# Two diffusion blocks on one core: diagonals of reciprocal sums in three attentions, and transposes of the weights in row halves in all four

## The chip, the core and the metric

The program runs on one core of one Trainium2 chip, as a single launch. The metric is the device time in microseconds of the whole program, the median over its runs. On the core, TensorE (PE) multiplies matrices and writes to PSUM, VectorE (DVE) and ScalarE (ACT) do the element-wise work, GpSimd (POOL) does a little of it, and SyncE (SP) issues most of the transfers. Each engine works through its own list of instructions in order and waits on semaphores.

## The reference, cut to what matters

Two blocks of two layers each are computed one behind the other, all in float32. Each layer holds one attention, four in all: a global one with grouped keys ("even"), one with a window and a sink ("odd"), one with low-rank keys ("mla") and a neighbourhood attention ("na"). All four have this core:

```python
def attend(q, k, v):
    s = jnp.einsum('bqhgd,bkhd->bhgqk', q, k).astype(jnp.float32)
    p = jax.nn.softmax(s, axis=-1).astype(v.dtype)
    return jnp.einsum('bhgqk,bkhd->bqhgd', p, v)
```

The odd one adds a mask and a sink column to the softmax; na adds a table of biases:

```python
    s = softmax_with_sink(jnp.concatenate([s_win, s_ctx], axis=-1))
    ...
    logits = jnp.concatenate([s_loc.reshape(B, H, GRID_W, n_loc), s_ctx], axis=-1)
    p = jax.nn.softmax(logits, axis=-1).astype(v.dtype)
```

There are 256 latent tokens and 256 context tokens. Heads have 64 channels.

## The kernel before

The feed-forward and projection stages multiply weights that stream in from HBM, each split into a high and a low part (three products, L522 to L524; in some stages two, L530 to L533). They take most of the time and aren't touched.

An attention is worked off in units. A unit (`attention_pairs`) is 128 queries of two heads: 16 units for even, odd and mla, 8 for na. Its keys are 256 or 512 (even and mla: 8 units of either), 384 (odd) or 512 (na). A unit passes through these steps, and the code of every engine loops over `it`, with different steps of different units in one iteration:

- scores, TensorE, L1519, unit `it`: two products, one for each head b, into banks 0 to 3; in even, odd and na they contract over 64 channels, head 0 in the rows 0 to 63 of the array and head 1 in rows 64 to 127; in mla over 128;
- row maximum, VectorE, L1577, unit `it` (odd and na first add mask or bias, L1571 and L1575);
- exponential, ScalarE, L1654, with the sums of the rows;
- reciprocal of the sums and scaling of the weights by it, VectorE, `scale_weights`, unit `it - 1`: L1598, then two TENSOR_SCALAR at L1602 over all keys; its last one lets TensorE go on (`probs_scaled`);
- transposes of the weights, TensorE, L1530, unit `it - 2`: one for each head and each block of 128 keys, so 4, 6 or 8, each 128x128, against an identity. Head b goes to bank 4 + b;
- copy of both banks to SBUF, ScalarE, L1640; it also gates the next unit's transposes (`turned_copied`), since the two banks aren't doubled;
- product of values and weights ("mix"), TensorE, L1548, unit `it - 3`, and the copy of its result (L1617 on VectorE, L1630 on ScalarE for odd), which the mix of a later unit waits for.

In the order of TensorE an iteration is scores of `it`, transposes of `it - 2`, mix of `it - 3`. A float32 product appears in the trace as two MATMUL instructions, each with its own weight load; a transpose is one.

Other work shares the stretches. Beside the even attention VectorE and ScalarE prepare the decays of the recurrent layer (L2677, L2683, L2529 to L2531). The odd one runs beside the last eight projection tiles (24 products of 256 columns each) with their splits (L422, L427) and rotations (L1793, L1817 to L1823), and its last part beside the first output tiles (L532, L533). Behind the attentions TensorE goes on with the recurrent layers (from L2335 and L3384 on) or the output projection.

The shapes on the array matter below: the trace writes 64*128 for a product that contracts over 64 rows and has 128 output rows, 128*64 for the mixes, 128*128 for the rest. L2414, in the recurrent layer, already transposes in row halves, and L3384 has float32 products of 64 rows with 128 columns of weights and 128 moving columns.

## Time and profile before

| | us |
|---|---|
| Median of 3 runs | 2491.78 (2486.28 to 2492.4) |
| The profiled execution, its own time | 2487.92 |
| Its span | 2486.1 |
| TensorE busy in the span | 2385.2 (96%) |
| VectorE busy | 1712.9 (69%) |
| ScalarE busy | 1062.8 (43%) |
| Even attention, first scores to the next layer's first product | 50.8 |
| Odd attention with the projection tiles beside it | 78.4 |
| MLA attention | 53.3 |
| Neighbourhood attention | 35.2 |

A busy TensorE isn't one at its peak: products are pipelined and their ends are modelled. Where it is busy all the time, the distance between the starts of two groups says what a group costs. The chain that ended last lies on TensorE for 83% of the span and on VectorE for 8%.

### The profile page before, as it was taken

To read this page: it belongs to the slowest core of one execution; us is meant where nothing else is said; L and a number is where in the kernel's file an instruction comes from. 1 tells how busy PE (TensorE), PEld (TensorE's weight loads), DVE (VectorE), ACT (ScalarE), POOL (GpSimd) and SP (SyncE) were. 2 spreads that over 40 slices of the span, in tenths; PEclk is the share of its full clock that TensorE was granted. 3 is DMA by queue.
4 is the path that set the end of the run, shared out by engine and by line. 5 is a ranking of instruction groups with operands and counts; after the bars stand their busy time and mean duration, and the time that the engine had idled before them with its cause. 6 is when DMAs were issued, how large, how long until landed. Compare 5 with 4: busy or idle time off the path is not lost.

```text
span 2486.1 us, 45211 instructions
## 1 busy us (share of the span) xinstructions
PE 2385.2 (96%) x17410; PEld 1922.4 (77%) x17410; DVE 1712.9 (69%) x2826; ACT 1062.8 (43%) x1748; POOL 380.5 (15%) x350
## 2 busy tenths in 40 slices
PE   6999999998888999999999999989999999999998
PEld 4888888866776878888788888767888885678877
DVE  3877787666565787778887763687777324776666
ACT  4232224356444622322523222475556334656354
POOL 2000001022444200000100001101002711211052
PEclk9999999999999999999999999999999999999999
DMA  7655663210000365566465553315564222113311
GB/s 294 225 194 191 194 201 125 93 39 3 4 4 19 104 215 194 192 194 203 144 216 193 191 176 99 109 38 161 186 184 138 90 97 91 31 52 128 117 45 52
DMA packets 89012, 324.76 MB, mean 131 GB/s; under 512 B 9888, under 2 KB 11040, under 8 KB 88096
## 3 DMA queue, kind: packets, MB, share of 16 engines
q1 hardware_dynamic: 86768, 310.15, 38.3%
q0 software_dynamic: 2096, 12.55, 1.5%
q8 instruction: 103, 1.69, 0.3%
q14 instruction: 45, 0.37, 0.0%
HBM read 321.49 MB, written 1.18 MB: 130 GB/s over the span
## 4 chain that ended last, share of the span: by engine, by line
PE 83%; DVE 8%; issue 3%; ACT 3%; DMA 1%; DVEq 1%; POOLq 0%; POOL 0%; ACTq 0%; SPq 0%
PE bank L522 20%; PE bank L523 20%; PE bank L524 20%; PE bank L532 5%; PE bank L533 3%; PE bank L1519 1%; DVE row_statistics L1577 1%; PE bank L1548 1%; PE bank L1530 1%; DMA projections<-stream_k 1%; DVE weights_hi_lo L427 1%; DVE work L1602 1%; PE bank L2414 1%; PE bank L1969 1%; PE bank L531 1%
## 5 line engine op out<-in xcount | busy, mean ns | idle before, releaser
L422 ACT ACTIVATE weights_hi_lo<-weight_ring 128x1024 fp32r<-128x1024 f32 (+1 forms) x338 | 352.2, 1042 | 992.0 <-PE bank L524 933.9
L522 PE MATMUL bank<-input_hi,weights_hi_lo 128*128 128x512 f32 (+1 forms) x1688 | 643.2, 381 | 12.3 <-DVE input_lo L866 4.5
L427 DVE TENSOR_TENSOR weights_hi_lo<-weight_ring,weights_hi_lo 128x1024 fp32r<-128x1024 f32 (+1 forms) x333 | 403.4, 1211 | 351.4 <-ACT weights_hi_lo L422 349.8
L523 PE MATMUL bank<-input_lo,weights_hi_lo 128*128 128x512 f32 (+1 forms) x1688 | 639.8, 379 | 0.0
L524 PE MATMUL bank<-input_hi,weights_hi_lo 128*128 128x512 f32 (+1 forms) x1688 | 639.5, 379 | 0.0
L522 PEld LDWEIGHTS bank<-input_hi,weights_hi_lo 128*128 128x128 f32 x1688 | 318.8, 189 | 79.0 <-issue 16.0
L524 PEld LDWEIGHTS bank<-input_hi,weights_hi_lo 128*128 128x128 f32 x1688 | 318.8, 189 | 59.6
L523 PEld LDWEIGHTS bank<-input_lo,weights_hi_lo 128*128 128x128 f32 x1688 | 318.8, 189 | 59.3 <-issue 0.7
L806 POOL TENSOR_TENSOR work<-work 128x512 f32<-128x512 f32 (+1 forms) x48 | 68.4, 1426 | 1225.2 <-ACT work L691 1224.3
L598 DVE CUSTOM_DVE_ANT_0 work<-weight_ring,extra_tiles 128x1024 f32<-128x1024 f32 x176 | 224.5, 1275 | 35.8 <-issue 13.2
L522 PE MATMUL bank<-hidden_hi_lo,weights_hi_lo 128*128 128x512 f32 x632 | 246.8, 390 | 0.0
L524 PE MATMUL bank<-hidden_hi_lo,weights_hi_lo 128*128 128x512 f32 x632 | 245.9, 389 | 0.0
L523 PE MATMUL bank<-hidden_hi_lo,weights_hi_lo 128*128 128x512 f32 x632 | 245.9, 389 | 0.0
L599 DVE CUSTOM_DVE_ANT_0 weight_ring<-weight_ring,extra_tiles 128x1024 f32<-128x1024 f32 x176 | 214.8, 1220 | 0.0
L522 PEld LDWEIGHTS bank<-hidden_hi_lo,weights_hi_lo 128*128 128x128 f32 x632 | 118.7, 188 | 25.1 <-ACT work L2780 0.2
L523 PEld LDWEIGHTS bank<-hidden_hi_lo,weights_hi_lo 128*128 128x128 f32 x632 | 118.7, 188 | 25.0 <-issue 0.5
L524 PEld LDWEIGHTS bank<-hidden_hi_lo,weights_hi_lo 128*128 128x128 f32 x632 | 118.6, 188 | 24.7
L1577 DVE TENSOR_REDUCE row_statistics<-bank 128x2 f32<-128x1024 f32 (+2 forms) x56 | 55.7, 994 | 26.2 <-PE bank L1519 24.1
L1397 DVE TENSOR_TENSOR work<-work,bank 128x512 f32<-128x512 f32 x66 | 45.4, 688 | 37.0 <-PE bank L524 32.9
L427 DVE TENSOR_TENSOR hidden_hi_lo<-weight_ring,hidden_hi_lo 128x1024 fp32r<-128x1024 f32 (+1 forms) x45 | 53.9, 1197 | 15.2 <-ACT hidden_hi_lo L422 14.9
L717 DVE SCALAR_TENSOR_TENSOR input_lo<-residual_stream,modulation,input_hi 128x256 fp32r<-128x256 f32 x96 | 58.4, 649 | 7.4 <-ACT input_hi L706 3.8
L691 ACT ACTIVATE work<-residual_stream 128x512 f32<-128x512 f32 (+1 forms) x72 | 40.9, 577 | 51.5 <-DVE residual_stream L1120 22.8
(598 smaller groups left out, 3725.2 us busy)
## 6 DMA issues: line engine op xcount, KB each, us to landing
weight_ring<-stream_k SPq DMA_DIRECT2D x481, 512.0 KB, 3.4
weight_ring<-stream_f SPq DMA_DIRECT2D x64, 448.0 KB, 3.4
weight_ring<-stream_f SPq DMA_DIRECT2D x32, 512.0 KB, 3.7
projections<-stream_k SPq DMA_DIRECT2D x14, 512.0 KB, 6.5
extra_tiles<-condrows POOLq DMA_DIRECT2D x3, 1024.0 KB, 8.2
constants<-consts POOLq DMA_DIRECT2D x1, 2112.5 KB, 8.3
residual_stream<-xin SPq DMA_DIRECT2D x1, 2048.0 KB, 10.4
work<-nabias POOLq DMA_DIRECT2D x1, 2048.0 KB, 9.3
```

The costliest lines, as they stand in the source:

```text
L422: act.activation(split_place(place)[:, 0, 0:words], w[:, 0:words], ACT.Copy).then_inc(hi_ready, 1)
L427: eng.tensor_tensor(split_place(place)[:, 1, 0:words], ring[:, n % RING, 0:words], split_place(place)[:, 0, 0:words].bitcast(F32), ALU.sub ...
L522: pe.matmul(out, weights[:, 0, w], x_hi, start=first, stop=False)
L523: pe.matmul(out, weights[:, 0, w], x_lo, start=False, stop=False)
L524: return pe.matmul(out, weights[:, 1, w], x_hi, start=False, stop=last)
L532: pe.matmul(bank[:, :], weights[:, 0, w], x_lo_hi, start=first, stop=False)
L533: return pe.matmul(bank[:, TC:T], weights[:, 1, w], x_lo_hi[:, TC:T], start=False, stop=False)
L598: dve.tensor_tensor_reduce(PRODUCTS, w, COND[:, 0, :], 1.0, 0.0, ALU.mult, ALU.add, MOD_SUMS[:, j, 0:1])
L599: dve.tensor_tensor_reduce(w, w, COND[:, 1, :], 1.0, 0.0, ALU.mult, ALU.add, MOD_SUMS[:, j, 1:2]) .then_inc(mod_read, 1)
L717: ins = dve.scalar_tensor_tensor(out=H_LO[:, kt, p:q], in0=X[:, kt, p:q], scalar=MODS[:, scale + kt, s:s + 1], in1=H_HI[:, kt, p:q].bitcas ...
L806: pool.tensor_tensor(total, total, squares_of(place, kt)[:, a:b], ALU.add)
L1577: ins = dve.tensor_reduce(st[:, 0, :], sc[:, :, 0:nk], AX.X, ALU.max, negate=True)
```

## The change

In even, odd and na the weights are no longer scaled. VectorE builds, in place of L1602, two small matrices of 128x64: each row p of matrix b holds the reciprocal of the sum of query p and head b in column p mod 64 and zeros elsewhere (the product of the two triangular masks `iu` and `il` is a stacked 64x64 identity). TensorE then multiplies the unscaled weights by it, so that turning and scaling are one product. The product contracts over queries in two halves of 64 rows: half 0 in the array's upper rows, into bank 4, half 1 in its lower rows, into bank 5, 64 moving columns each. For mla the scaling stays, and the transposes are cut into the same halves against a 64x64 part of the identity. The copy of L1640 puts the halves together again as it writes; the mix reads the same columns from a flat tile.

Per unit with n blocks (n = 4, 6 or 8 for 256, 384 or 512 keys), TensorE had n transposes. It now has 2n products for even, odd and na, which are 4n MATMUL instructions, and 2n transposes for mla.

```diff
--- before.py
+++ after.py
@@ -387,7 +387,7 @@
         scores_ready = sem("scores_ready")
         max_ready = sem("row_max_ready")
         probs_ready = sem("probs_ready")
-        probs_scaled = sem("probs_scaled")
+        probs_scaled = sem("probs_scaled_or_diagonals_ready")
         probs_turned = sem("probs_transposed")
         turned_copied = sem("transposed_probs_copied")
         mixed = sem("values_mixed")
@@ -1476,7 +1476,20 @@
 
         def attention_turned(which, u):
 
-            return BIG[:, 16 + u % 2 * 2:18 + u % 2 * 2, :] if which == "odd" else WORK[:, 20 + u % 2 * 2:22 + u % 2 * 2, :]
+            two = BIG[:, 16 + u % 2 * 2:18 + u % 2 * 2, :] if which == "odd" else WORK[:, 20 + u % 2 * 2:22 + u % 2 * 2, :]
+            return two.rearrange("p b t -> p (b t)")
+
+        def turned_halves(ap):
+
+            return ap.rearrange("p (i h c) -> p h i c", h=2, c=HD)
+
+        QUERY_HALVES = [slice(HD * i, HD * i + HD) for i in range(2)]
+        BY_DIAGONALS = ("even", "odd", "na")
+
+        def sum_diagonals(which, u):
+
+            tile = {"even": BIG[:, 29, 0:TC], "odd": BIG[:, 24, TC:T], "na": SPARE[:, 6, 0:TC]}[which]
+            return tile[:, u % 2 * P:u % 2 * P + P].rearrange("p (b c) -> p b c", b=2)
 
         def mix_bank(which, u):
 
@@ -1525,9 +1538,17 @@
                     pe.wait_ge(probs_scaled, u0 + u + 1)
                     if u >= 1:
                         pe.wait_ge(turned_copied, u0 + u)
+                    nt = len(key_tiles(which, pairs[u][1]))
                     for b in range(2):
-                        for i in range(len(key_tiles(which, pairs[u][1]))):
-                            mm = pe.transpose(pb[4 + b][:, tok(i)], attention_probs(which, u)[:, b, tok(i)], C("ident"))
+                        for i in range(nt):
+                            o = slice((b * nt + i) * HD, (b * nt + i + 1) * HD)
+                            for h, half in enumerate(QUERY_HALVES):
+                                weights = attention_probs(which, u)[half, b, tok(i)]
+                                if which in BY_DIAGONALS:
+                                    mm = pe.matmul(pb[4 + h][:, o], weights, sum_diagonals(which, u)[half, b, :], start=True,
+                                                   stop=True)
+                                else:
+                                    mm = pe.transpose(pb[4 + h][:, o], weights, C("ident")[half, half])
                     mm.then_inc(probs_turned, 1)
                 u = it - 3
                 if 0 <= u < n:
@@ -1546,7 +1567,8 @@
                         for b in range(2):
                             ch = attention_operands(which, t, b, qt)[2]
                             mm = pe.matmul(mix_bank(which, u)[HD * b:HD * b + HD, 0:P], attention_values(which, tile, ch),
-                                           attention_turned(which, u)[:, b, tok(i)], start=i == 0, stop=i == len(keys) - 1)
+                                           attention_turned(which, u)[:, tok(b * len(keys) + i)], start=i == 0,
+                                           stop=i == len(keys) - 1)
                     mm.then_inc(mixed, 1)
                     if which == "odd" and u == n - 1:
                         odd_out_half(pe, 1, range(KT - 1))
@@ -1597,6 +1619,12 @@
                         dve.drain()
                 dve.reciprocal(st[:, 1, :], st[:, 4, :])
                 dve.drain()
+                if which in BY_DIAGONALS:
+                    for b in range(2):
+                        ins = dve.scalar_tensor_tensor(out=sum_diagonals(which, u)[:, b, :], in0=C("iu"), scalar=st[:, 1, b:b + 1],
+                                                       in1=C("il"), op0=ALU.mult, op1=ALU.mult)
+                    ins.then_inc(probs_scaled, 1)
+                    return
                 for b in range(2):
                     probs = attention_probs(which, u)[:, b, 0:nk]
                     ins = dve.tensor_scalar(probs, probs, st[:, 1, b:b + 1], None, ALU.mult)
@@ -1637,7 +1665,8 @@
                     act.wait_ge(probs_turned, u0 + u + 1)
                     if u >= 2:
                         act.wait_ge(mixed, u0 + u - 1)
-                    act.activation(attention_turned(which, u)[:, :, 0:nk], banks[:, 4:6, 0:nk], ACT.Copy).then_inc(turned_copied, 1)
+                    act.activation(turned_halves(attention_turned(which, u)[:, 0:2 * nk]),
+                                   banks[:, 4:6, 0:nk].rearrange("p h (i c) -> p h i c", c=HD), ACT.Copy).then_inc(turned_copied, 1)
                 if which == "odd" and it in ODD_SLAB_BESIDE:
                     odd_slab_hi(act, ODD_SLAB_BESIDE[it])
                 if it < n:
```

On TensorE, in the even attention at the first units with 512 keys, before:

```order
L1519 MATMUL bank<-projections 128x512 x2
L1530 MATMUL bank<-constants,work 128x128 x4
L1548 MATMUL bank<-work,projections 64x128 x4
L1519 MATMUL bank<-projections 128x512 x2
L1530 MATMUL bank<-constants,work 128x128 x8
L1548 MATMUL bank<-work,projections 64x128 x4
```

and now, with L1532 the scores, L1548 the turning and L1569 the mix:

```order
L1532 MATMUL bank<-projections 128x512 x2
L1548 MATMUL bank<-projections,work 128x64 x8
L1569 MATMUL bank<-work,projections 64x128 x4
L1532 MATMUL bank<-projections 128x512 x2
L1548 MATMUL bank<-projections,work 128x64 x16
L1569 MATMUL bank<-work,projections 64x128 x4
```

The row counts a product once; the shape is output rows by moving columns. Nothing has moved past anything: eight transposes have become sixteen products of half the width.

On VectorE, at the same units, before:

```order
L1577 TENSOR_REDUCE row_statistics<-bank 128x2
L1598 RECIPROCAL row_statistics<-row_statistics 128x2
L1602 TENSOR_SCALAR work<-work,row_statistics 128x512 x2
L1617 COPY mixer_io<-bank 128x128
L1577 TENSOR_REDUCE row_statistics<-bank 128x2
L1598 RECIPROCAL row_statistics<-row_statistics 128x2
L1602 TENSOR_SCALAR work<-work,row_statistics 128x512 x2
```

and now, with L1599 the maximum, L1620 the reciprocal and L1645 the copy of the mix:

```order
L1599 TENSOR_REDUCE row_statistics<-bank 128x2
L1620 RECIPROCAL row_statistics<-row_statistics 128x2
L1624 SCALAR_TENSOR_TENSOR projections<-constants,row_statistics 128x64 x2
L1645 COPY mixer_io<-bank 128x128
L1599 TENSOR_REDUCE row_statistics<-bank 128x2
L1620 RECIPROCAL row_statistics<-row_statistics 128x2
L1624 SCALAR_TENSOR_TENSOR projections<-constants,row_statistics 128x64 x2
```

The pair of scalings over all keys has become a pair of operations over 64 columns, in the same place of the order.

## Rows read from the trace of the kernel before

**Rows 1.** The page, first part: busy us (share of the span), instructions.
```profile
PE 2385.2 (96%) x17410; PEld 1922.4 (77%) x17410; DVE 1712.9 (69%) x2826; ACT 1062.8 (43%) x1748; POOL 380.5 (15%) x350
```

**Rows 2.** The four attention stretches: length, busy us of each engine, granted clock, DMA.
```profile
533.69:584.50 50.81, 42.87 (x361) 27.40 (x360) 40.85 (x93) 35.14 (x87) 14.64 (x13) 0.97 0.03 7
1603.99:1682.34 78.35, 70.51 (x534) 51.44 (x534) 63.18 (x172) 48.75 (x132) 0.00 (x0) 0.96 0.15 48
2106.17:2159.47 53.30, 50.45 (x377) 34.26 (x376) 34.13 (x84) 34.99 (x86) 2.82 (x5) 1.00 0.08 26
2377.78:2412.93 35.15, 31.43 (x289) 21.48 (x289) 29.71 (x52) 27.28 (x52) 30.15 (x64) 1.00 0.01 1
```

**Rows 3.** Waits of TensorE, even stretch (us, times, longest), and three in its timeline.
```profile
PE bank L1530 <- DVE work L1602: 6.1, 6, 2.5
...
539.07 0.94 PE L1530 MATMUL bank<-constants,work 128*128 128x128 f32 x4 [1.12 <-DVE work L1602]
...
550.48 1.09 PE L1530 MATMUL bank<-constants,work 128*128 128x128 f32 x8 [1.89 <-DVE work L1602]
...
561.35 0.88 PE L1530 MATMUL bank<-constants,work 128*128 128x128 f32 x6 [2.46 <-DVE work L1602]
```

**Rows 4.** Waits of TensorE, odd stretch.
```profile
PE bank L1530 <- DVE projections L1602: 4.4, 5, 1.9
PE bank L522 <- DVE projections L1823: 3.5, 3, 1.9
PE bank L1548 <- ACT projections L1630: 1.0, 2, 0.8
```

**Rows 5.** Waits of TensorE, MLA stretch, then neighbourhood stretch.
```profile
PE bank L1530 <- DVE work L1602: 0.8, 3, 0.3
...
PE bank L1530 <- DVE work L1602: 2.2, 4, 1.0
...
PE bank L1530 <- ACT work L1640: 0.5, 1, 0.5
```

**Rows 6.** Timeline of TensorE, even stretch: start, us, engine, line, counts.
```profile
544.05 0.66 PE L1530 MATMUL bank<-constants,work 128*128 128x128 f32 x4
...
555.50 0.70 PE L1519 MATMUL bank<-projections 64*128 64x256 f32 x4
556.14 1.09 PE L1530 MATMUL bank<-constants,work 128*128 128x128 f32 x8
557.16 1.09 PE L1548 MATMUL bank<-work,projections 128*64 128x128 f32 x16
```

**Rows 7.** Row-half products of L3384: timeline of TensorE, then the weight loads by form.
```profile
2404.39 1.16 PE L3384 MATMUL bank<-work 64*128 64x128 f32 x16
...
2412.93 1.61 PE L3384 MATMUL bank<-work 64*128 64x128 f32 x24 [0.39 <-DVE mixer_io L1617]
...
L3384 PEld LDWEIGHTS bank<-projections 64*128 64x128 f32 x144 | 8.7, 187 | 0.7
```

**Rows 8.** Timeline of TensorE, transposes in row halves at L2414.
```profile
596.36 0.46 PE L2414 MATMUL bank<-constants,work 64*128 64x64 f32 x8 [0.23 <-ACT projections L2541]
596.75 0.70 PE L2407 MATMUL bank<-spare_tiles,work 64*64 64x64 f32 x32
```

**Rows 9.** VectorE by form: busy us, mean ns, idle before.
```profile
L1602 DVE TENSOR_SCALAR work<-work,row_statistics 128x512 f32<-128x512 f32 x48 | 23.7, 536 | 1.9
...
L1602 DVE TENSOR_SCALAR work<-work,row_statistics 128x256 f32<-128x256 f32 x32 | 11.0, 385 | 1.2
...
L1806 DVE SCALAR_TENSOR_TENSOR projections<-projections,constants 128x128 f32<-128x128 f32 x2 | 0.6, 284 | 0.0
```

**Rows 10.** Odd stretch, timeline of TensorE, and a window with its granted clock.
```profile
1660.93 0.87 PE L1530 MATMUL bank<-constants,projections 128*128 128x128 f32 x6
1665.39 1.29 PE L1530 MATMUL bank<-constants,projections 128*128 128x128 f32 x6 [1.93 <-DVE projections L1602]
...
1665.40:1669.00 3.60, 3.60 (x22) 2.54 (x22) 2.58 (x8) 1.86 (x6) 0.00 (x0) 0.54 0.00 0
```

## The prediction

> **What bounds the kernel now.** I read the page's first part, then the four attention stretches as windows, then TensorE's waits in each, then its timeline. The page has TensorE busy for 96% of the span [rows 1], so the question is what an attention costs TensorE, and where TensorE isn't the bound. In the windows [rows 2] TensorE is busy for 42.9 of 50.8 us in the even stretch, 70.5 of 78.4 in the odd one, 50.5 of 53.3 in mla and 31.4 of 35.2 in na. VectorE is busy for 40.9, 63.2, 34.1 and 29.7 of them: close behind in even and odd, far behind in mla. TensorE's waits say the same. It waits for the scaling of L1602 for 6.1 us in even, in six places, of 1.1, 1.9 and 2.5 us and three short ones [rows 3]; 4.4 us in odd, beside 3.5 for the rotations and 1.0 for a copy [rows 4]; only 0.8 in mla and 2.2 in na [rows 5]. So the scaling holds TensorE up for 13.5 us at most, 12.7 of them in the three attentions that lose it. The rest of the time TensorE pays for each of its instructions, and the change gives it more of them.
>
> **What a turning costs TensorE now.** Four transposes take 0.66 us and eight take 1.09 [rows 6]: 0.43 / 4 = 0.1075 for a block of 128 keys. From the start of the eight to the start of the mix it is 1.02 us = 8 x 0.1075 + 0.16. The 0.16 is lost where the shape on the array changes (128*128 to 128*64). The scores, 64*128, are followed by the transposes, 128*128, so such a change is paid there too: it is in the 0.64 us from 555.50 to 556.14. A third is paid from the mix to the next scores.
>
> **What it costs in the changed kernel (even, odd, na).** The new product has 64 rows and 128 columns of weights, as the scores have: so the change of shape behind the scores goes, minus 0.16 a unit. Each block becomes four instructions, two in each half of the rows, so two pairs. L3384 has just such pairs with 128 moving columns: 16 instructions take 1.16 us and 24 take 1.61 [rows 7], so 0.45 / 4 = 0.112 for a pair. Here the moving side is half as wide, but the weights are as wide, and a weight load takes 187 ns from start to end [rows 7], whichever product follows it. The price of a pair isn't in the trace. Bounds: L2414, row halves with 64 moving columns whose loads are those of transposes, needs 0.39 us for eight, less 0.16 for the shape, so 0.06 a pair [rows 8]; two loads one behind the other would be 0.187 x 2 = 0.37. I take 0.112, from the row with the same kind of load, since I think that there the loads set the pace as much as the products do.
>
> The Trainium skill, in "TensorE: Matmul & The Clock Gate", section "LDWEIGHTS (loading the stationary operand)", says that a load takes as long as its columns, and that fewer rows don't shorten it: 128 columns at 1.2 GHz, an estimate of 0.107 us for either half. By that rule the pair is 0.107 and the sum below becomes about 5 us. It speaks against the change, and no row here shows loads outlasting their products.
>
> For n blocks the difference is then n x (2 x 0.112 - 0.1075) - 0.16 = 0.1165 n - 0.16:
> - 4 blocks, plus 0.31; 6 blocks, plus 0.54; 8 blocks, plus 0.77.
> - Even: 8 x 0.31 + 8 x 0.77 = 8.6 us. Odd: 16 x 0.54 = 8.6. Na: 8 x 0.77 = 6.2. In all 23.4 us more on TensorE.
>
> **What VectorE saves.** Over 512 keys a scaling takes 0.54 us, over 256 0.39 [rows 9]. A scalar_tensor_tensor over 128 columns takes 0.28 [rows 9], so over 64 columns between nothing and 0.28; I take 0.22. Where two follow each other the second starts early, so a unit is ready about 0.5 us sooner with 512 keys, 0.4 with 384 and 0.3 with 256: 8 x 0.5 + 8 x 0.3 in even, 16 x 0.4 in odd, 8 x 0.5 in na, 16.8 us off VectorE. This counts only where TensorE waits, and the longer turning fills the same gaps: a wait can go once, not twice.
> - Even: the first wait (1.1 us, the pipeline filling) stays nearly whole. The two long ones (1.9 and 2.5) come after VectorE's extra work for the decays. By the first TensorE has five units of turning behind it (1.5 us more) and VectorE is 1.3 us ahead; by the second all slack is used up. Of 6.1 us I give back 5.0. Net: 8.6 - 5.0 = plus 3.6.
> - Odd: here VectorE sets the period as often as TensorE. Of 4.4 + 1.0, and 1.3 of the 3.5 for rotations (the other 2.2 lie before any turning) 6.7 us, plus some 0.15 us six times in which the turning starts late without a listed wait, 0.9, I give back 6.3. Net: plus 2.3.
> - Na: two units fill the pipeline behind other transposes. Of 2.2 and the 0.5 behind a copy [rows 5] I give back 2.0. Net: plus 4.2.
>
> **The clock in odd.** At 1665.4, behind a wait of 1.93 us, the granted clock is 0.54 over 3.6 us: the 1.2 GHz level for most of it. Six transposes take 1.29 us there in place of 0.87 [rows 10]. TensorE is busy for all of the 3.6 us, so it loses 3.6 x 0.46 = 1.6. By my count the wait ahead of it shrinks below 0.5 us, so the fall goes: minus 1.6. Bounds: none of it, or all.
>
> **Mla.** A block is one pair of half transposes, 0.06 in place of 0.1075, but the shape now changes behind the scores (128*128) too: 0.16 - 0.0475 n, so minus 0.03 with 4 blocks and minus 0.22 with 8. Over 8 of each: minus 2.0 us, with TensorE the bound.
>
> **At nothing.** ScalarE's copy reads the same columns and writes them in another order; in odd, even and na it waits for TensorE before most copies. The diagonals' tiles are free at these places; nothing waits for them anew. Stages behind an attention start when TensorE leaves it, so a shift there passes on whole. No transfer is moved.
>
> **Sum.** 3.6 + (2.3 - 1.6) + 4.2 - 2.0 = plus 6.5 us. The profiled execution, 2487.9 us, would take 2494.4; it lies 3.9 below the median shown, 2491.8, so the median becomes 2498.3: 0.26% more. A measurement here can tell about 0.3% (7.5 us) from no change, so the likeliest verdict is "same", on its slow side.
>
> **Rivals.**
> - A, faster. The pair costs what the half transposes do, 0.06, because loads in both halves and under the running products hide. Then n x (0.12 - 0.1075) - 0.16 is negative: minus 0.11, 0.085 and 0.06 for 4, 6 and 8 blocks, which is 1.4 us less in even, 1.4 in odd and 0.5 in na. The waits shrink by a quarter of 12.7, since VectorE's other work stays: 3.2. With mla's 2.0 that is minus 8.5, 2483. It decides below a pair of about 0.09. For it: the moving side is halved, and rows 8. Against it: 187 ns of load. The Trainium skill's "TensorEngine Tiling (Array Packing)", section "Theoretical Speedup", promises up to twofold for a contraction of 64 rows or fewer; by that rule this rival holds. 10%.
> - B, slower. The waits don't give way: TensorE's longer turning delays the copy of L1640, this the mix and the next turning, so a unit's chain grows by more than VectorE saved. Then the 23.4 us stand against only a third of the 13.3 that I gave back, and mla's 2.0: 23.4 - 4.4 - 2.0 = plus 17, 2509. It decides from a return of under 8 us on. For it: single banks 4 and 5. Against it: TensorE is busy between waits already. 12%.
> - C, the loads of the two halves don't overlap at all: 0.19 to 0.37 a pair, at 0.19 plus 0.27 n - 0.16 a unit, 2.0 with 8 blocks: over 40 us. L3384's pairs at 0.112 contradict it. 3%.
> - D, the forecast: pair of 0.107 to 0.12, plus 4 to plus 11 us. 75%.
>
> **The numbers.** In D the middle is plus 6.5 with a spread of 3.5 from the pair, the waits, the clock and the runs' own scatter, so it lies above 7.5 in four cases of ten: 0.30 slower, 0.45 same. A gives 0.05 faster and 0.05 same; B and C 0.15 slower, of which B leaves 0.01 same. Together: faster 0.05, same 0.51, slower 0.44. The range holds D and the near edges of A and B: 2489 to 2508.
>
> **What would show it.** Eight-block turnings at 1.85 to 2.0 us from their start to that of the mix; under 0.5 us, not 0.64, from the start of 256-key scores to the turning. Waits for the diagonals below 2.5 us in even and below 2 in odd. The stretches at about 54.4, 79.1, 51.3 and 39.4 us. In mla turnings at 0.65 us where eight blocks took 1.0. I am wrong if an eight-block turning takes under 1.3 us (A), or if the turning takes what I say and the stretches grow by more than 7 us each (B).

## The result, and the profile after

| | kernel before | changed kernel |
|---|---|---|
| median of 8 runs | 2491.57 us | 2496.94 us |
| lowest, highest | 2486.28, 2492.40 | 2494.84, 2502.63 |
| profiled execution, span | 2486.1 | 2494.3 |

The ratio of the runs is 1.0029, 95% interval 1.0018 to 1.0039: 5.4 us slower, where 6.5 were forecast (2498.3 us, range 2489 to 2508). The profiled executions lie 8.2 us apart. That is 2.8 more than the medians, since the one of before was 3.7 us under its median and the one of after 0.8: the profile of before is of a quick execution, and what the profiles below show is more than what the medians do.

The page's first part and the four attention stretches of the changed kernel (columns as in [rows 1] and [rows 2]; from the same instruction to the same instruction):

```profile
PE 2409.2 (97%) x18274; PEld 1958.2 (79%) x18274; DVE 1700.0 (68%) x2826; ACT 1062.1 (43%) x1748; POOL 376.2 (15%) x350
...
531.67:588.36 56.69, 53.05 (x650) 41.97 (x649) 35.97 (x93) 34.90 (x87) 13.36 (x13) 0.94 0.03 7
1608.00:1687.95 79.95, 76.81 (x822) 63.61 (x823) 59.37 (x172) 47.75 (x132) 0.00 (x0) 0.98 0.15 48
2111.70:2162.59 50.89, 47.71 (x473) 30.49 (x472) 33.89 (x84) 35.00 (x86) 2.75 (x5) 1.00 0.09 28
2382.43:2421.24 38.81, 37.35 (x480) 29.74 (x480) 26.79 (x52) 27.33 (x52) 28.31 (x66) 1.00 0.01 2
```

Set against [rows 2], length and TensorE's busy time give this ledger (us; idle is length less busy):

| stretch | length | forecast | busy | forecast | idle | forecast |
|---|---|---|---|---|---|---|
| even | +5.9 | +3.6 | +10.2 | +8.6 | -4.3 | -5.0 |
| odd | +1.6 | +0.7 | +6.3 | +7.0 | -4.7 | -6.3 |
| mla | -2.4 | -2.0 | -2.7 | -2.0 | +0.3 | 0 |
| na | +3.7 | +4.2 | +5.9 | +6.2 | -2.3 | -2.0 |
| all | +8.7 | +6.5 | +19.7 | +19.8 | -10.9 | -13.3 |

Outside the four, the program before the even stretch was 2.0 us quicker in this execution (no code of it is changed), the stage between mla and na 1.5 us slower (below, the clock), and the rest within 0.15: 8.7 - 2.0 + 1.5 = 8.2 us.

TensorE's timeline in the even stretch shows the turning at its new price, beside [rows 6]. L1532 is the scores, L1548 the turning, L1569 the mix:

```profile
546.63 1.00 PE L1548 MATMUL bank<-projections,work 64*128 64x64 f32 x16
547.57 0.66 PE L1569 MATMUL bank<-work,projections 128*64 128x128 f32 x8
...
549.78 2.00 PE L1548 MATMUL bank<-projections,work 64*128 64x64 f32 x32 [0.49 <-DVE projections L1624]
551.71 0.66 PE L1569 MATMUL bank<-work,projections 128*64 128x128 f32 x8
...
556.15 0.70 PE L1532 MATMUL bank<-projections 64*128 64x256 f32 x4
556.68 1.90 PE L1548 MATMUL bank<-projections,work 64*128 64x64 f32 x32
558.51 1.09 PE L1569 MATMUL bank<-work,projections 128*64 128x128 f32 x16
```

From its start to that of the mix, four blocks take 0.94 us and eight take 1.83: (1.90 - 1.00) / 8 = 0.1125 for a pair, where 0.112 was forecast. The whole turning was forecast at 1.85 to 2.0 us; one that has just waited takes 0.10 more (1.93). From the 256-key scores to the turning it is 0.53 us; it was 0.64, and under 0.5 was forecast.

TensorE's waits in the even stretch, then in odd, then in na, beside [rows 3 to 5]: L1624 makes the diagonals.

```profile
PE bank L1548 <- DVE projections L1624: 1.9, 3, 1.0
PE bank L1532 <- ACT projections L1743: 0.9, 1, 0.9
...
PE bank L522 <- DVE projections L1852: 2.8, 3, 1.9
PE bank L1548 <- DVE projections L1624: 1.1, 2, 0.6
PE bank L1569 <- ACT projections L1658: 0.5, 1, 0.5
...
PE bank L1548 <- ACT work L1668: 0.3, 1, 0.3
PE bank L1548 <- DVE spare_tiles L1624: 0.2, 1, 0.2
```

The 12.7 us of waits for the scaling are 3.2 us of waits for the diagonals. A diagonal takes VectorE 0.30 us in the mean in even and odd and 0.41 in na, not 0.22:

```profile
L1624 DVE SCALAR_TENSOR_TENSOR projections<-constants,row_statistics 128x64 f32<-128x64 f32 x64 | 16.5, 300 | 2.4
...
L1624 DVE SCALAR_TENSOR_TENSOR spare_tiles<-constants,row_statistics 128x64 f32<-128x64 f32 x16 | 5.9, 408 | 0.6
```

So VectorE's busy time in the three stretches falls by 133.7 - 122.1 = 11.6 us, not by 16.8.

### The profile page after: what moved, and what is told of

It is laid out like the page before. It is cut to its first block, busy times and chain, and to the rows that moved or that the text cites. A ratio compares the mean times of both kernels' runs of the same rounds, so it can differ in the third digit from the quotient of the medians.

```text
span 2494.3 us, 46939 instructions
## 1 busy us (share of the span) xinstructions
PE 2409.2 (97%) x18274; PEld 1958.2 (79%) x18274; DVE 1700.0 (68%) x2826; ACT 1062.1 (43%) x1748; POOL 376.2 (15%) x350
## 4 chain that ended last, share of the span: by engine, by line
PE 85%; DVE 6%; issue 3%; ACT 3%; DMA 1%; DVEq 1%; POOLq 0%; POOL 0%; ACTq 0%; SPq 0%
PE bank L522 20%; PE bank L523 20%; PE bank L524 20%; PE bank L532 5%; PE bank L533 3%; PE bank L1548 2%; PE bank L1532 2%; PE bank L1569 1%; DMA projections<-stream_k 1%; PE bank L3413 1%; PE bank L2443 1%; PE bank L1998 1%; PE bank L531 1%; PE bank L3448 1%; DVE row_statistics L1599 1%
## 5 line engine op out<-in xcount | busy, mean ns | idle before, releaser
L1599 DVE TENSOR_REDUCE row_statistics<-bank 128x2 f32<-128x1024 f32 (+2 forms) x56 | 55.7, 994 | 32.3 <-PE bank L1532 30.4
```

The lines of the kernel that those rows point to most:

```text
L1599: ins = dve.tensor_reduce(st[:, 0, :], sc[:, :, 0:nk], AX.X, ALU.max, negate=True)
```

## The experiments

All variants start from the changed kernel. Two things were made separate: whether TensorE turns by a product or by a transpose, and whether VectorE makes diagonals or scales the weights. Ratios are to the kernel before, with their 95% interval.

### What sets the price of a pair: the product or the load

Narrow moving sides:

```
-  mm = pe.matmul(pb[4 + h][:, o], weights, sum_diagonals(which, u)[half, b, :], ...)
+  mm = pe.matmul(pb[4 + h][:, o.start:o.start + 32], weights, sum_diagonals(which, u)[half, b, 0:32], ...)
```

> The changed kernel with moving sides of 32 columns in place of 64 in the products of even, odd and neighbourhood (half of the queries are left out of the output). Loads are as in the changed kernel, products half as wide. Theory (the loads set the pace; L3384's pairs with 128 moving columns cost 0.112 us as well): an eight-block turning stays at 1.83 to 1.93 us from its start to that of the mix, a pair at 0.112. Rival (the products' columns count): the pair falls to 0.06 to 0.08 and the turning to 1.05 to 1.35 us.

Narrow weights:

```
-  mm = pe.matmul(pb[4 + h][:, o], weights, sum_diagonals(which, u)[half, b, :], ...)
+  mm = pe.matmul(pb[4 + h][0:HD, o], weights[:, 0:HD], sum_diagonals(which, u)[half, b, :], ...)
```

> The changed kernel with weights of 64 columns in place of 128 in the same products (half of the keys of each block are left out of the output), moving sides of 64 columns as in the changed kernel. Theory (the loads set the pace): the pair falls to about 0.06 us, since half as many columns are loaded, and an eight-block turning to 1.0 to 1.2 us; the mix's instructions, with weights of 64 columns and 128 moving ones, need 0.0625 each. Rival (a fixed cost of an instruction of about 0.056, whatever it loads): the turning stays at 1.83 to 1.93 us.

The first leaves half of the queries out of the output, the second half of the keys of each block. TensorE's timeline in na, first with narrow moving sides:

```profile
2414.85 1.87 PE L1554 MATMUL bank<-spare_tiles,work 64*128 64x32 f32 x32
2416.65 1.09 PE L1574 MATMUL bank<-work 128*64 128x128 f32 x16
```

and with narrow weights:

```profile
2381.01 1.15 PE L1554 MATMUL bank<-spare_tiles,work 64*64 64x64 f32 x32
2382.09 1.09 PE L1574 MATMUL bank<-work 128*64 128x128 f32 x16
```

Half as many moving columns: 1.80 us to the mix in place of 1.83, so next to nothing. Half as many columns of weights: 1.08 us. The price of a pair again comes from turnings of four and of eight blocks, here with narrow weights in even:

```profile
567.44 0.68 PE L1554 MATMUL bank<-projections,work 64*64 64x64 f32 x16
569.70 1.15 PE L1554 MATMUL bank<-projections,work 64*64 64x64 f32 x32
```

(1.15 - 0.68) / 8 = 0.059 for a pair. With narrow moving sides the same two turnings take 0.98 and 1.87 us: 0.111. So the width of the weights sets the price of a product's pair, and it is 0.11 us with 32 and with 64 moving columns, as it is with 128 at L3384 [rows 7]. The rule that the prediction drew from the Trainium skill ("TensorE: Matmul & The Clock Gate", section "LDWEIGHTS (loading the stationary operand)") gave 0.107 for 128 columns, and half of it for 64; the runs agree within some 5% for 128 and show 0.059 for 64.

Width alone doesn't make the price, though. The half transposes in mla of the changed kernel load 128 columns into either half too, and a pair of them costs (0.71 - 0.46) / 4 = 0.0625. Their loads are shorter, 138 ns from start to end beside 188 for a product's (two turnings by transposes, then the loads of a transpose and of a product):

```profile
2124.41 0.71 PE L1551 MATMUL bank<-constants,work 64*128 64x64 f32 x16
2127.99 0.46 PE L1551 MATMUL bank<-constants,work 64*128 64x64 f32 x8
...
L1551 PEld LDWEIGHTS bank<-constants,work 64*128 64x128 f32 x192 | 7.2, 138 | 9.9 <-issue 6.5 <-DVE work L1630 3.5
L1548 PEld LDWEIGHTS bank<-spare_tiles,work 64*128 64x128 f32 x256 | 15.3, 188 | 4.2 <-issue 1.6 <-DVE spare_tiles L1624 1.6 <-ACT spare_tiles L2061 1.0
```

That it is the load, and not something else that goes with the width of the weights (the rows of the result are halved with it), is argued from this, not shown. Why a product's load is dearer than a transpose's is open.

With narrow moving sides the kernel took 2513.53 us, with narrow weights 2476.80 (one run each). The first is far slower than the changed kernel, though it does the same loads and half the columns. The clock shows why, in a stretch in which TensorE was busy without a gap:

```profile
540.00:574.00 34.00, 34.00 (x242) 26.81 (x242) 17.46 (x40) 15.86 (x40) 5.12 (x5) 0.50 0.01 1
```

It was granted the 1.2 GHz level for 34 us on end, where the changed kernel was for 6.8. The kernel ran again:

> Products with moving sides of 32 columns once more (half of the queries left out of the output). The first look took 2513.53 us, and TensorE's granted clock was 0.50 for 34 us of the even stretch, in which it was busy without a gap; with 64 columns the same stretch has it at 0.50 for 3.4 or 6.8 us. Theory (how much a product moves counts for the clock, not only whether TensorE is busy): the clock stays low for over 15 us in even again, stretch at 62 us or more, ratio to the kernel before 1.005 or more. Rival (a chance of that execution): at most 7 us at the lower level, stretch at 55 to 57 us, ratio 1.002 to 1.004.

The ratio is 1.0058 [1.0041, 1.0074], against 1.0024 and 1.0029 for 64 columns. The even and the odd stretch:

```profile
534.00:591.38 57.38, 53.95 (x650) 42.90 (x649) 36.56 (x93) 34.54 (x87) 13.24 (x13) 0.91 0.03 7
1611.15:1697.96 86.81, 84.10 (x822) 70.42 (x823) 59.34 (x172) 47.96 (x132) 0.00 (x0) 0.88 0.17 50
```

In even the clock was low for 10 us this time, not for the 15 of the theory, and the stretch took 57.4 us, so the 34 us were in part a chance of that execution, as the rival had it. But in odd the granted clock is 0.88, 0.98 with 64 columns, and that stretch is 6.9 us longer (79.95 with 64); in the first execution it was 0.92 there. The ratio is the theory's, and its interval lies above both of the changed kernel's. So narrower products save no time, and the clock stood lower with them in both executions, once for 34 us in which TensorE never waited; how much it costs in one place differs from execution to execution. Why they cost clock is open.

### Whole products in place of row halves

VectorE scales here, and the moving side is a constant identity; mla stays in halves. Shown against the whole transpose of the kernel before; the copy is again that of the kernel before too.

```
-  mm = pe.transpose(pb[4 + b][:, tok(i)], attention_probs(which, u)[:, b, tok(i)], C("ident"))
+  mm = pe.matmul(pb[4 + b][:, tok(i)], attention_probs(which, u)[:, b, tok(i)], C("ident"), start=True, stop=True)
```

> Products with a constant identity over all 128 rows at once in place of row halves, in even, odd and neighbourhood, VectorE scales; mla in halves. One load of 128 columns now serves 128 moving columns. Theory (a load of 128 columns takes 0.056 us beside another of its pair, and in whole tiles 0.107 as L3448's instructions show with 0.107 to 0.11 each): two instructions a block, 0.215 us, an eight-block turning 1.75 to 1.95 us to the mix, so the row halves of the change gain nothing; ratio 1.003 as with row halves and scaling. Rival (whole products are bound by their columns and cost twice): turning over 2.5 us, ratio over 1.008.

Its ratio is 1.0050 [1.0035, 1.0066]. TensorE's timeline in na:

```profile
2406.74 1.13 PE L1534 MATMUL bank<-projections 64*128 64x512 f32 x4
2407.80 2.05 PE L1547 MATMUL bank<-constants,work 128*128 128x128 f32 x16
2409.78 1.09 PE L1575 MATMUL bank<-work 128*64 128x128 f32 x16
```

An eight-block turning takes 1.98 us to the mix, against 1.83 in row halves, and the scores ahead of it hold 1.06 us in place of 0.96. The row halves are worth 0.25 us of 3.04 a unit: 0.10 between scores and turning, 0.15 between the turning's start and the mix. None of it is in the price of a block, as four and eight blocks in even show:

```profile
576.31 1.16 PE L1547 MATMUL bank<-constants,work 128*128 128x128 f32 x8
579.05 2.05 PE L1547 MATMUL bank<-constants,work 128*128 128x128 f32 x16
```

A block is two instructions, so (2.05 - 1.16) / 4 = 0.2225 us, beside 2 x 0.1125 = 0.225 in halves. All of the 0.25 is paid once a unit, where the shape on the array changes. The up to twofold of the Trainium skill ("TensorEngine Tiling (Array Packing)", section "Theoretical Speedup"), by which rival A held, doesn't show here for products. For the transposes much of it does: 0.0625 for a block in halves, 0.1075 whole [rows 6], although either half loads 128 columns there too. The theory's turning was a little short (1.75 to 1.95), and its ratio of 1.003 too low; its rival's 2.5 us and 1.008 are out.

### What VectorE's saving is worth with long turnings

```
-  side = sum_diagonals(which, u)[half, b, :]      # and VectorE makes the diagonals
+  side = C("ident")[half, half]                   # and VectorE scales the weights, as before
   mm = pe.matmul(pb[4 + h][:, o], weights, side, start=True, stop=True)
```

> TensorE turns by products in row halves, as in the changed kernel, but against a constant identity, and VectorE scales the weights, as before. This takes VectorE's saving (16.8 us by the prediction) away from the change and leaves TensorE's work. Theory (what the change gives back comes half from the diagonals' earlier readiness, half from longer turnings that fill gaps): waits for the scaling 6 to 8 us in the three stretches (12.7 before, 3.2 in the changed kernel), 12 to 16 us over the kernel before, ratio 1.0055. Rival 1 (longer turnings alone fill the gaps): as the changed kernel, 5 to 8 us over the kernel before, ratio 1.003. Rival 2 (turnings delay the copies and the waits stay): plus 20 us and more, ratio 1.008.

> Products against a constant identity with VectorE's scaling, once more. It measured 1.0031 [1.0017, 1.0044], the changed kernel 1.0029 and 1.0024. Theory (the diagonals' earlier readiness is worth 1 to 3 us, since the longer turnings fill most waits by themselves): ratio 1.0028 to 1.0038. Rival (it is worth the 8 us of waits that the prediction counted for VectorE's saving): over 1.005.

The two gave 1.0031 [1.0017, 1.0044] and 1.0038 [1.0025, 1.0052]: rival 1 of the first expectation, longer turnings alone fill the gaps, came nearer than my theory (1.0055). The waits for the scaling that this theory expected, 6 to 8 us, are there: 6.3 and 6.1 us in the two profiles. The changed kernel gave 1.0029, and once more:

> The changed kernel itself, on the same chip as the one with whole transposes in mla, for comparison of medians and as a second look at where the clock falls. Theory: ratio 1.0029 as measured before, within 1.0018 to 1.0039; the even stretch between 53.5 and 57 us, according to whether the clock falls for 3.4 or 6.8 us behind the first wait. Rival (the length of that fall belongs to the changed kernel): 6.8 us again and 56.7 us.

1.0024 [1.0015, 1.0034]. So all of VectorE's saving is worth about 0.0008 of the ratio, 2 us; by the differences of the medians it is 3.7. The intervals overlap, so the ratios alone don't tell it from nothing. The stretches even, odd and na with products and scaling (second execution profiled):

```profile
534.38:593.18 58.80, 53.70 (x649) 41.79 (x648) 41.06 (x93) 34.87 (x87) 13.70 (x13) 0.94 0.02 7
1610.24:1690.05 79.81, 75.64 (x822) 62.37 (x822) 63.43 (x172) 47.92 (x132) 0.00 (x0) 1.00 0.15 48
...
2383.08:2422.28 39.20, 37.35 (x481) 29.74 (x481) 29.39 (x52) 27.31 (x52) 30.56 (x66) 1.00 0.01 2
```

TensorE idles for 5.1, 4.2 and 1.9 us: 11.1 in all. It was 19.5 before and is 8.2 in the changed kernel. So of the 11.3 us of idle time that went, 8.4 go without any saving on VectorE, by the longer turnings alone, and the diagonals bring 2.9. The other profile with scaling has 11.2; the second one of the changed kernel has 8.9, which makes 2.3 of the 2.9.

The second profile of the changed kernel bears on what the even stretch owes to the clock. Its even stretch and its odd one:

```profile
533.59:589.41 55.82, 51.58 (x650) 40.59 (x649) 35.96 (x93) 35.02 (x87) 13.35 (x13) 0.97 0.02 7
1605.96:1686.20 80.24, 77.09 (x822) 63.97 (x822) 59.37 (x172) 47.74 (x132) 0.00 (x0) 0.98 0.15 48
```

With the granted clock at 0.97, as in [rows 2], even is 5.0 us longer than before: TensorE 8.7 us busier (8.6 forecast) and 3.7 less idle (5.0 forecast). The other 0.9 us of the first profile were its clock, 0.94. So the longer fall doesn't come every time. But it isn't rare: the changed kernel with whole transposes in mla (below) has the same even stretch, and the clock was low for 6.8 us there again:

```profile
533.55:590.46 56.91, 53.06 (x649) 41.96 (x649) 35.97 (x93) 34.91 (x87) 13.37 (x13) 0.94 0.02 7
```

That is two of three executions, and with products and scaling the fall lasted 10.2 and 6.8 us. Of the four kernels that turn by transposes and scale, none has a fall of over 3.4 us in even. Whole products, on the other hand, have none at all. So the theory's range for the stretch held, but its rival, that the longer fall belongs to the changed kernel, isn't out: these few profiles leave it open.

### Short turnings: with scaling, with diagonals, and with fillers

No products: transposes in row halves in all four attentions, VectorE scales.

```
-  BY_DIAGONALS = ("even", "odd", "na")
+  BY_DIAGONALS = ()
```

> The transposes in row halves stay, in all four attentions, but VectorE scales the weights again, as in the kernel before; no diagonals. Theory (a turning costs what the rows of mla in the changed kernel show, 0.0625 us for a pair, and no change of shape behind 64-row scores, 0.10 to 0.16): TensorE saves 0.045 us a block and 0.10 to 0.16 a unit in even, odd and neighbourhood, up to 15 us in all, but VectorE's scaling ends as late as before, so waits take back two thirds of it. With mla's 2.4 us the kernel takes 6 to 10 us less than the one before, ratio 0.9965. Turnings of eight blocks at 0.65 us instead of 1.02, waits for the scaling in the three stretches 20 us or more (12.7 before). Rival 1 (TensorE is the bound between waits): ratio 0.9935, 15 us less. Rival 2 (all of it turns into waits outside mla): 2.4 us less, ratio 0.999.

The same turnings, but VectorE makes the diagonals and nothing is scaled:

```
-  if which in BY_DIAGONALS:
-      mm = pe.matmul(pb[4 + h][:, o], weights, sum_diagonals(which, u)[half, b, :], start=True, stop=True)
-  else:
-      mm = pe.transpose(pb[4 + h][:, o], weights, C("ident")[half, half])
+  mm = pe.transpose(pb[4 + h][:, o], weights, C("ident")[half, half])
```

> VectorE makes the diagonals instead of the scaled weights, but TensorE turns with half transposes against the identity; the reciprocal sums are thus left out of the output of even, odd and neighbourhood attention. It shows what VectorE's saving is worth with short turnings. Theory (VectorE or TensorE sets the period): both saved, waits 8 to 12 us in the three stretches, 14 to 18 us less than the kernel before, ratio 0.9935. Rival (the chain of a unit, scores, maximum, exponential, copy, sets the period now, or ScalarE does): no more than 10 us less, ratio 0.996, with waits for ScalarE over 5 us in place of those for VectorE.

The first again, with work for TensorE ahead of its waits (the wait for the last copy, `turned_copied`, is moved ahead of this work, since it writes to bank 4):

```
+  if which != "mla" and u >= 1:
+      for i in range(4):
+          pe.transpose(pb[4][:, tok(i)], C("ident"), C("ident"))
   pe.wait_ge(probs_scaled, u0 + u + 1)
```

> The kernel with half transposes and scaled weights everywhere, and ahead of each wait for the scaling in even, odd and neighbourhood four whole transposes of the identity, whose result is overwritten: TensorE works where it waited. That kernel waited 21.6 us for the scaling in the three stretches, and its clock was at the lower level for 57 us in all, 31 in the kernel before. Theory (the falls come from waits; they gave back what the faster turnings gained): with fillers the lower level lasts under 35 us in all, the stretches lose 4 to 6 us of half-clock time and pay for the fillers outside waits, 37 units of 0.43 to 0.75 us less the waits, 4 to 8 us; whole kernel within 3 us of the one without fillers. Rival (the falls don't depend on these waits): lower level at 50 us or more, and the kernel 4 to 10 us slower.

With all runs beside each other, TensorE's busy and idle time summed over even, odd and na of the profiled executions (us):

| turning | VectorE | ratio | busy | idle | length |
|---|---|---|---|---|---|
| whole transposes (before) | scales | 1 | 144.8 | 19.5 | 164.3 |
| half transposes | scales | 0.9996 [0.9987, 1.0005] | 134.5 | 29.7 | 164.1 |
| half transposes, fillers | scales | 1.0000 [0.9991, 1.0009] | 150.9 | 14.8 | 165.7 |
| half transposes | diagonals | 0.9970 [0.9958, 0.9983] | 133.9 | 23.7 | 157.6 |
| products in halves | scales | 1.0038 [1.0025, 1.0052] | 166.7 | 11.1 | 177.8 |
| products in halves (the change) | diagonals | 1.0029 [1.0018, 1.0039] | 167.2 | 8.2 | 175.4 |
| whole products | scales | 1.0050 [1.0035, 1.0066] | 170.7 | 9.5 | 180.3 |

Without the products TensorE works 10.3 us less, and idles 10.2 more: what it saves outside mla turns into waits for VectorE. They are 21.6 us for the scaling, in even, odd and na, where the kernel before had 12.7:

```profile
PE bank L1556 <- DVE work L1635: 9.8, 10, 2.2
...
PE bank L1556 <- DVE projections L1635: 7.2, 8, 2.2
...
PE bank L1556 <- DVE work L1635: 4.6, 7, 1.4
```

Of the three expectations for that kernel rival 2 (0.999) came nearest, and my theory (0.9965) fell. With VectorE's saving and short turnings the kernel takes 0.3% less, 7 us, which its rival came nearer to (0.996) than my theory (0.9935): 2.9 us of the waits in na are then for ScalarE's copy, and 4.1 in odd, as the rival said, beside 11.2 in the three stretches for the diagonals. So VectorE does bound these stretches before, and its saving is worth 6 to 7 us with short turnings, but 2 to 4 behind products that have filled its waits already.

No version with the full output is faster than the kernel before by more than a measurement can tell: the best are the two with 0.9996.

The fillers cost 16.4 us of TensorE's time in the three stretches and lengthen them by 1.5. The odd stretch even gets shorter by 1.7 us, first without fillers, then with them:

```profile
1603.39:1682.92 79.53, 67.65 (x631) 51.22 (x631) 63.21 (x172) 48.61 (x132) 0.00 (x0) 0.91 0.16 54
```

```profile
1605.98:1683.82 77.84, 71.53 (x694) 52.66 (x696) 63.42 (x172) 48.26 (x132) 0.00 (x0) 1.00 0.15 49
```

The granted clock is 0.91 where TensorE idles for 11.9 us and 1.00 where it idles for 6.3. But one of the falls without fillers, 3.4 us, lies at the very start of this stretch, ahead of any turning of odd. Kernels with the same code there have it or lack it (the one before has it, the one with whole products doesn't). It is worth 1.5 of the 1.7 us. From the first scores of odd on, again without and with fillers:

```profile
1609.09:1682.92 73.83, 62.43 (x606) 46.52 (x605) 61.80 (x170) 47.55 (x131) 0.00 (x0) 0.93 0.15 51
...
1610.18:1683.55 73.37, 67.53 (x665) 49.20 (x664) 62.01 (x170) 47.20 (x131) 0.00 (x0) 1.00 0.14 45
```

So the fillers paid for themselves in odd, no more. In the record of the clock the lower level lasts 17 us in the three stretches without fillers (that one fall included) and 3.4 with them; over the whole program it is 57 and 41 us (31 before), between what the theory (under 35) and the rival (50 or more) had said, as the rest of the falls lie elsewhere. All executions say the same: the mean granted clock is 0.9885 in the eleven without fillers, 0.9925 in the eleven with them, and 0.993 in those of the kernel before beside either. The whole kernel is 1.0 us slower than without fillers by the ratios, 2.0 by the medians, each set against the kernel before that ran beside it. That is within the theory's 3, and within the noise.

### Mla's part

Whole transposes outside mla, halves in mla: the kernel before with mla's part of the change alone.

```
-  mm = pe.transpose(pb[4 + h][:, o], weights, C("ident")[half, half])
+  mm = pe.transpose(pb[4 + b][:, tok(i)], attention_probs(which, u)[:, b, tok(i)], C("ident"))   # even, odd, na
```

> The kernel before, with transposes in row halves in mla alone: the part of the change that the prediction put at minus 2.0 us. Theory: the mla stretch at 50.9 us as in the changed kernel (53.3 before), whole kernel 2 us less, ratio 0.9991 with the rest the same. Rival (the clock falls of the changed kernel at 2169 and 2179 us, behind mla, belong to the shorter mla): the 2.4 us are given back in the stage behind it, ratio 1.000.

And the changed kernel with whole transposes in mla alone:

> The changed kernel with whole 128x128 transposes in mla again, diagonals and products elsewhere as they are: it takes mla's part away from the change. Theory (the shorter mla stretch is worth its 2.4 us, of which the clock falls behind it give back half or more): mla stretch 53.3 us, no clock falls at 2169 and 2179, the whole kernel 0 to 1.5 us over the changed one, ratio to the kernel before 1.0030 to 1.0035. Rival 1 (mla's gain counts whole): plus 2.4 us over the changed kernel, ratio 1.0039. Rival 2 (falls cost more than the stretch gains): below the changed kernel, ratio 1.0024 or less.

The first has ratio 0.9996 [0.9987, 1.0005], 0.7 us less by its median. The second has 1.0032 [1.0019, 1.0044], 2.9 us over the changed kernel that ran beside it (2499.24 and 2496.34). Both signs are those forecast for mla, but neither difference is clear of noise: the first interval holds 1, and the second overlaps that of the changed kernel. The first stands between its theory (0.9991) and its rival (1.000); the second lies in the theory's range by its ratio and nearer rival 1 by its median. So the size, 0.7 to 2.9 us, isn't settled. In the profiles the mla stretch is 53.3 us with whole transposes in both kernels that have them. With halves it is 50.9, or 52.4 to 52.8 where the clock falls near its start, as in the first of these two.

Behind mla, the changed kernel does the same work with the same waits as the kernel before, and is 1.5 us slower. TensorE's timeline there, before:

```profile
2164.91 2.47 PE L3111 MATMUL bank<-projections,work 128*128 128x129 f32 x20 [2.59 <-DVE work L3013]
...
2175.12 2.47 PE L3111 MATMUL bank<-projections,work 128*128 128x129 f32 x20 [2.04 <-DVE work L3038]
```

and in the changed kernel:

```profile
2168.03 3.44 PE L3140 MATMUL bank<-projections,work 128*128 128x129 f32 x20 [2.59 <-DVE work L3042]
...
2179.03 4.11 PE L3140 MATMUL bank<-projections,work 128*128 128x129 f32 x20 [2.04 <-DVE work L3067]
```

The waits are equal to a hundredth, 2.59 and 2.04 us, but behind them the granted clock fell in one execution and not in the other. The whole stage, before and then after:

```profile
2159.47:2377.78 218.31, 207.14 (x1138) 173.57 (x1137) 146.87 (x300) 114.10 (x201) 33.15 (x21) 1.00 0.30 102
```

```profile
2162.59:2382.43 219.84, 209.95 (x1139) 176.28 (x1137) 146.79 (x300) 114.11 (x201) 33.18 (x21) 0.98 0.31 101
```

The rival of the first kernel of this part, that the two falls belong to the halves in mla, has this for it: both are in seven of the twelve profiled executions with halves there (in the changed kernel's both times), and in neither of the two with whole ones (one of these, the changed kernel with whole transposes in mla, has one fall, 218.6 us). Against it: with products and scaling, both times, and with narrow weights or sides, mla was in halves and the stage had no fall and took 218.3 us. One or two profiles of each kernel don't tell whether the halves or the moment at which the stage begins decides. That stays open.

## Why the prediction was right, step by step

- **The price of a pair** was right, 0.1125 measured for 0.112, and so was its reason as far as it was tested: the width of the weights counts and the moving side doesn't, shown by narrow weights and narrow moving sides. Rival A (0.06) and rival C (over 0.19) are gone with that. The step from a pair of 0.107 to "about 5 us" is slightly off: 0.01 us less a block, over 256 blocks, takes 2.6 from 6.5, so with the returns unchanged it is about 4.
- **The shape** was mis-sized. It was put at 0.16 us ahead of the turning and again behind it. It is 0.10 to 0.11 ahead (0.53 for 0.64; 0.96 for 1.06), and behind a product turning that hadn't waited 0.03 (1.83 less 16 x 0.1125), 0.13 behind one that had. A unit of eight blocks costs 0.70 more than before where 0.77 was forecast. The sum of busy time still came out at 19.7 for 19.8, because the longer fall of the clock put 1.5 us into even (10.2 less the 8.7 of the second profile).
- **The waits that go** were the step that was too high: 13.3 us given back, 10.9 measured, 1.3 of it short in even by the second profile and 1.6 in odd. In even I had counted the long waits as gone, and 1.9 to 2.5 us of waits for diagonals stay. The reason I gave was right only in part: three quarters of what went are gaps that the longer turnings filled, one quarter or a little less is VectorE's saving. This saving was itself too high, as a diagonal takes 0.30 to 0.41 us and not 0.22.
- **The clock in odd**: the fall behind the 1.93 us wait is gone in both profiles of the changed kernel; its largest wait for a diagonal in odd is 0.6 us. The granted clock over the stretch rose from 0.96 to 0.98, not to 1.00, as the fall at its start stayed. What the sum lacked is that the clock is in play in every other place too: a longer fall in even and two behind mla, 2.4 us in this profile; the two behind mla are in the second profile too.
- **Na**: 3.7 for 4.2, and 38.81 us in both profiles. **Mla**: 2.4 us for 2.0 where no fall came in, 0.9 where one did; its turnings of eight blocks are 0.64 us, as forecast.
- **Rival B** (waits don't give way) is out: idle time fell by more than half. Three stretches grew, by 1.6 to 5.9 us, none by 7.
- **At nothing**: ScalarE's busy time is 1062.1 us for 1062.8, and nothing new waits for its copy.

So the forecast of 6.5 us beside the measured 5.4 is a sum with a right price for the product and four terms off by up to 2.5 us, whose errors partly cancel: the waits, mla's gain, the clock, and the scatter between the executions. That it came within 1.1 us is in part luck. In the two profiles of the changed kernel the four stretches grew by 8.7 and 9.7 us, not by 6.5, and the stage behind mla by 1.5 more; other stages, whose code is the same, were quicker by 2.1 and 2.4, and the profile of before is of an execution quicker than its median. The interval of the ratio, 1.0018 to 1.0039, is 4.5 to 9.7 us: it bears out the sum, not each of its terms.

## What to carry to other kernels

Replacing a transpose by a float32 product turns one instruction into two with a full load each; if the weights stay 128 columns wide, making the moving side or the contraction smaller buys nothing a block, so price it by rows with weights as wide and of the same kind: a product's pair costs 0.1125 us, a half transpose's 0.0625, with 128 columns of weights in both. Work taken off the engine that is waited for counts only after the waits that the other half of the change fills by itself: here some 2 to 4 us of 11.6, which two runs of each kernel don't yet set apart from nothing. Before counting on a shorter stage in a kernel with waits, look at the granted clock: the 10.3 us that short turnings saved came back as idle time, and the mean granted clock went from 0.993 to 0.9885.

## What the runs showed of the hardware that was not expected

- Halving the moving columns from 64 to 32 left a turning at 1.80 us, yet made the kernel 0.3% slower (1.0058 for 1.0024 to 1.0029): the granted clock was 0.75 and 0.91 in even (0.94 and 0.97 with 64 columns) and 0.92 and 0.88 in odd (0.98 twice), once at the 1.2 GHz level for 34 us in which TensorE had no gap.
- The same instructions behind the same wait of 2.59 us took 2.47 us in one execution and 3.44 in another: the wait alone doesn't decide whether the clock falls.
- 16.4 us of useless transposes in front of waits cost the kernel 1 to 2 us, within the noise, with a mean granted clock of 0.9925 in place of 0.9885 over eleven executions of each.
- In row halves with 128 columns of weights, a transpose's pair costs 0.0625 us and a product's 0.1125; whole, a block is 0.1075 by a transpose and 0.2225 by a product. Halving the rows pays for transposes and not for products.
